# The row of the MLP's inverse roots by two DMA transfers over DRAM, in a hybrid decoder layer on one core

## The chip, the cores and the metric

The kernel runs on one core of a Trainium2 chip. The metric is the device time of one execution in microseconds (us), lower is better.

## The reference

One decoder layer on x of 512 tokens by 1024 channels, in float32. The mixer (block-sparse attention and a gated delta rule side by side) is untouched here. What matters is the second half:

```python
x = x + rms_norm(y, post_norm_mix[l])          # y is the mixer's output
h = rms_norm(x, pre_norm_mlp[l])               # x * rsqrt(mean(x*x) + eps) * gain
y = jnp.square(jax.nn.relu(h @ w_mlp_in[l])) @ w_mlp_out[l]
x = x + rms_norm(y, post_norm_mlp[l])
```

with w_mlp_in 1024 x 4096 and w_mlp_out 4096 x 1024.

## The kernel before, in words

All engines have a program written out by hand, tied together by semaphores. The weights come in units of 128 x 512 elements (256 KB each). SP loads a unit into one of four slots of `raw` (L442), ACT copies it rounded into `w_hi` (`split`, through the helper `copy` on L906), POOL subtracts to get the rest `w_lo` (L1550), and PE multiplies each unit in three passes (hi by hi, hi by lo, lo by hi: L494 to L496 in `three`). The slots are reused with u % 4: ACT's split of unit u waits until PE is done with unit u-4, and runs three units ahead of PE (LEAD = 3).

In the MLP the hidden layer is computed transposed: channels of the hidden layer on the partitions, the 512 tokens along the row. The norm's inverse root is one number for each token, so it isn't applied to h. It is applied after the product, in `relu` on DVE (L1209 by the helper `stt`): `relu_sb = max(bank, 0) * rs_row`. For this `rs_row` must hold the 512 roots as one row of 2 KB, the same on each of the 128 partitions. POOL computes the roots the other way round: `rs2`, 128 partitions by 4, where token t*128+p sits on partition p in column t (`root_x2`: L1543, L1544, then the semaphore `rs2_ready`).

The kernel before turns one into the other in three steps. DVE multiplies the 128 x 128 identity by each column of `rs2` to four diagonal blocks `rs_diag` (L1488, semaphore `diag_ready`). PE multiplies a matrix of ones with `rs_diag` into bank 7 (L847, semaphore `row_full`); the profile shows it as two matmuls. ACT copies bank 7 to `rs_row` (L906, semaphore `row_ready`), and DVE's first relu waits for that.

I number the units of w_mlp_in here as m0, m1, ... (m0 is U_OUT of the code). m0 to m3 are the first block of 256 hidden channels, computed in two halves of the tokens into banks 4 and 5. m4 to m7 are the second block, into banks 2 and 3; each such unit is 12 matmuls of 512 columns. The product with ones stands in PE's program after m6 (`first and j == 2` in `mlp_in`). m8 opens the third block, in banks 0 and 1, and before it PE waits for `relu_done` >= 2, that is for DVE's first two relu instructions, which need `rs_row`.

ACT's program around it (`mlp_in(0, True)`, by its j): splits of m4 and m5 between the squares of x; then j=3 splits m6, j=4 splits m7, j=5 splits m8 (it waits for PE to end m4), j=6 splits m9 (waits for m5), j=7 waits for the product with ones, copies `rs_row`, squares the first two relu results (L1145), then splits m10. On POOL the order is: lo of m4 and m5, the root `root_x2`, lo of m6, and so on. DVE has nothing else to do between the last h_lo and the first relu but the four diagonals. SP's queue carries only the loads of the units there.

Of the kernel before, what the change touches and what calls it, by code (L numbers as in the profile page):

```python
# [16 lines left out]
F32 = mybir.dt.float32  # L17
F32R = mybir.dt.float32r
ALU = mybir.AluOpType
# [3 lines left out]
P = 128  # L23
D = 1024
S = 512
NT = S // P
# [141 lines left out]
def program(nc, x, pre_norm_mix, w_in, conv_w, a_log, dt_bias, dn_norm, w_branch_att, w_branch_dn, w_out,  # L168
# [5 lines left out]
    def at(name, kb, shape, dt=F32):  # L174
        return nc.alloc_sbuf_tensor_at(name, shape, dt, offset=base + int(kb * KB))
# [53 lines left out]
    a_hi = at("a_hi", 176, [P, 4, S], F32R)  # L229
    a_lo = at("a_lo", 184, [P, 4, S], F32R)  # L230
    relu_sb = at("relu_sb", 56, [P, 4, S])
    rs_diag = at("rs_diag", 64, [P, NT, P])
    rs_row = at("rs_row", 66, [P, S])
    y_out = at("y_out", 56, [P, NT, D])

# [2 lines left out]
    def small(name, shape, dt=F32):  # L238
        n = 4
        for d in shape[1:]:  # L240
            n *= d
        t = nc.alloc_sbuf_tensor_at(name, shape, dt, offset=base + off[0])
        off[0] += (n + 31) // 32 * 32
        return t

    ident = small("ident", [P, P])
    neg = small("neg", [P, P])
    ones = small("ones", [P, P])
# [40 lines left out]
    rs2 = small("rs2", [P, NT])  # L289
# [3 lines left out]
    bank = [ctx.enter_context(nc.psum_tensor(f"bank{i}", [P, 512], F32)) for i in range(8)]  # L293
    side = bank[4:]

    def sem(name):
        return ctx.enter_context(nc.semaphore(name))
# [73 lines left out]
    y_scaled = sem("y_scaled")  # L371
    ss2_ready = sem("ss2_ready")
    rs2_ready = sem("rs2_ready")
    diag_ready = sem("diag_ready")
    row_full = sem("row_full")
    row_ready = sem("row_ready")
    t2_full = sem("t2_full")
    t2_hi = sem("t2_hi")
    t2_lo = sem("t2_lo")
# [9 lines left out]
    pool_chain = sem("pool_chain")  # L389

    row_copy = nc.dram_tensor("row_copy", (32, P), F32).ap()
    w1 = w_in[0]
    xt = x[0].rearrange("(t p) d -> t p d", p=P)
    ot = out[0].rearrange("(t p) d -> t p d", p=P)
# [96 lines left out]
    def _(pe):  # L491
# [23 lines left out]
        def unit(u, toks=slice(0, S), done=True, own=None):  # L515
# [3 lines left out]
            if u < U_IN:  # L519
                g = UNIT_GROUP[u]  # L520
                first, banks, _, need = TABLE[g]
                j = u - first
                if GROUPS[g][1] == "f":
# [293 lines left out]
        def mlp_in_unit(s, b, toks):  # L817
            for kk in range(2):
                for m in range(2):
                    c = slice(kk * 256 + m * P, kk * 256 + m * P + P)  # L820
                    k = 2 * s + kk
                    x_ = three(bank[b + m][:, toks], w_hi[:, s, c], w_lo[:, s, c], h_hi[:, k, toks], h_lo[:, k, toks],
                               k == 0, k == KD - 1)
            return x_
# [13 lines left out]
        def mlp_in(i, first):  # L838
            for q in range(1 if first else 0, 2):
                if not first:  # L840
                    pe.wait_ge(relu_done, i * 4 + (2 * q - 2))
                for j in range(4):
                    pe.wait_ge(lo_ready, i * 8 + (U_OUT + 4 * q + j + 1))
                    mlp_in_unit(j, 2 * q, slice(0, S)).then_inc(unit_done, 1)
                    if first and j == 2:
                        pe.wait_ge(diag_ready, NT)
                        pe.matmul(bank[7][:], ones[:], rs_diag[:], start=True, stop=True).then_inc(row_full, 1)  # L847

        mlp_in(0, True)
        with pe.Fori(1, 8) as i:  # L850
            mlp_in(i, False)
# [36 lines left out]
    def _(a):  # L888
        n = {}

        def mark(i, s):

            n[s.name] = n.get(s.name, 0) + 1
            i.then_inc(s, 1)
            a.wait_ge(s, n[s.name])
# [9 lines left out]
        def copy(o, i_, scale=1.0):  # L905
            return a.activation(o, i_, ACT.Copy, scale=scale)  # L906
# [19 lines left out]
        def split(u, slot, loaded, used):  # L926

            a.wait_ge(raw_in[slot], loaded)
            if used is not None:
                a.wait_ge(unit_done, used)  # L930
            copy(w_hi[:, slot, :], raw[:, slot, :]).then_inc(hi_ready, 1)
# [24 lines left out]
        def side_step(name, i):  # L956
# [24 lines left out]
            elif name == "sg":  # L981
                a.wait_ge(conv_done, i + 1)
                dst = qk_dn[:, i, :] if i < 8 else v_dn[:, i - 8, :]
                mark(a.activation(dst, dst, ACT.Silu), silu_done if i < 8 else silu_v_done)
            elif name == "ev" and i in (10, 11):
                first, banks, _, _ = TABLE[i]
                for m, b in enumerate(banks):
                    if m < NT - 1:
# [152 lines left out]
        def square_group(i, q):  # L1141

            for m in range(2):
                a.wait_ge(relu_done, i * 4 + (2 * q + m + 1))
                a.activation(act[:, bass.ds(i * 4 + (2 * q + m), 1), :].rearrange("p a s -> p (a s)"), relu_sb[:, 2 * q + m, :],  # L1145
                             ACT.Square).then_inc(act_ready, 1)

        def mlp_in(i, first, last=False):
            for j in range(8):
                u = U_OUT + LEAD + j  # L1150
                if first and j == 7:
                    a.wait_ge(row_full, 1)
                    mark(copy(rs_row[:], bank[7][:]), row_ready)
                    square_group(i, 0)
                if not (first and j < 3):
                    split(None, u % 4, i * 32 + 16 * (u // 4 + 1), i * 8 + (u - 3))
                if last and j == 5:
                    act_hi(0, 0, False)
                    act_hi(0, 1, False)
                if j in (3, 7) and not (first and j == 3):  # L1160
                    square_group(i, j // 4)

        def act_hi(i, kt, used):

            a.wait_ge(act_ready, i * 4 + (kt + 1) if not isinstance(i, int) else 4 * i + kt + 1)
            if used:
                a.wait_ge(unit_done, i * 8 + (U_M1 + 2 * (kt - 4) + 2))
            copy(a_hi[:, kt % 4, :], act[:, bass.ds(i * 4 + kt, 1), :].rearrange("p a s -> p (a s)")).then_inc(ahi_ready, 1)

        mlp_in(0, True)  # L1170
        with a.Fori(1, 7) as i:
            mlp_in(i, False)
        mlp_in(7, False, True)

        def mlp_out(i, first, last):
# [16 lines left out]
    def _(v):  # L1192
        n = {}

        def mark(i, s):
            n[s.name] = n.get(s.name, 0) + 1
            i.then_inc(s, 1)
            v.wait_ge(s, n[s.name])
# [269 lines left out]
        def h2_part(half, ks):  # L1468
            toks = slice(256 * half, 256 * half + 256)
            for k in ks:  # L1470
                v.wait_ge(t2_hi, half * KD + k + 1)
                mark(stt(h_lo[:, k, toks], bank[k % 4][:, k // 4 * 256:k // 4 * 256 + 256], wmlp[:, k:k + 1],
                         h_hi[:, k, toks].bitcast(F32), ALU.mult, ALU.subtract), t2_lo)
# [9 lines left out]
        h2_part(0, range(6, 8))  # L1483
        residual(3)
        h2_part(1, range(8))
        v.wait_ge(rs2_ready, 1)
        for t in range(NT):
            mark(v.tensor_scalar(rs_diag[:, t, :], ident[:], rs2[:, t:t + 1], None, ALU.mult), diag_ready)  # L1488
        v.wait_ge(row_ready, 1)

        def relu(i, first=False, ms=range(4)):

# [209 lines left out]
```

## Time and profile before

| | us |
|---|---|
| three runs | 785.43, 785.59, 1565.65 |
| their median | 785.59 |
| the profiled execution's own time | 785.03 |
| its span | 783.3 |
| PE busy | 772.8 (99% of the span) |
| ACT, POOL, DVE busy | 354.5, 393.7, 330.5 |
| TensorE's granted clock, mean | 0.998 |

The span is what the profiler saw of the engines; the execution's own time is 1.7 us longer. A number such as L906 is a line of the kernel. PE is the matmul engine, PEld its weight loads, DVE VectorE, ACT ScalarE, POOL GpSimd, SP SyncE; a q behind the name is the engine's instruction queue, where DMAs are issued. Matmuls overlap in the record, so the distance between starts is the pace, not the duration.

### The profile page before, as it was taken

The numbers are of one execution on the slowest core, as the hardware profiler recorded it, in microseconds if no ns is written. First come the engines' busy times: TensorE is split into PE (matmuls) and PEld (weight loads), VectorE is DVE, ScalarE is ACT, GpSimd is POOL, SyncE is SP. The second block draws the span as 40 slices with busy tenths as digits, with TensorE's granted clock in tenths as the row PEclk, the third lists the DMA queues.
The fourth block names the chain that finished last, engine by engine and source line by source line (L and its number), as shares of the span: only waits on it lengthen the run. The fifth ranks groups of instructions, "written<-read, shape, count | busy, mean of one in ns | idle before, by whom it ended". The sixth has DMA issues, their size and how long they took to land.

```text
span 783.3 us, 12452 instructions
## 1 busy us (share of the span) xinstructions
PE 772.8 (99%) x4355; PEld 636.5 (81%) x4355; DVE 330.5 (42%) x502; ACT 354.5 (45%) x633; POOL 393.7 (50%) x347
## 2 busy tenths in 40 slices
PE   9999999999999999999999999999999999999996
PEld 8688788888887878888888888888888888888885
DVE  3596979881463545454507411110113222122225
ACT  6646861268555446445326633333334333333333
POOL 4446994434356343574446454445444544444444
PEclk9999999999999999999999999999999999999999
DMA  6236233323212121223732233333332322332222
GB/s 222 68 94 203 56 82 93 95 81 82 69 41 71 53 69 46 91 77 99 257 97 77 81 95 93 94 107 94 94 93 94 108 95 94 100 100 95 94 80 108
DMA packets 60026, 75.18 MB, mean 96 GB/s; under 512 B 6056, under 2 KB 45008, under 8 KB 59984
## 3 DMA queue, kind: packets, MB, share of 16 engines
q1 hardware_dynamic: 59776, 74.34, 31.5%
q8 instruction: 26, 0.43, 0.2%
q10 hardware_dynamic: 208, 0.28, 0.1%
q14 instruction: 16, 0.13, 0.1%
HBM read 72.49 MB, written 2.11 MB: 95 GB/s over the span
## 4 chain that ended last, share of the span: by engine, by line
PE 95%; DVE 2%; ACT 1%; issue 1%; POOL 1%; DMA 1%; ACTq 0%; DVEq 0%; POOLq 0%
PE bank L494 29%; PE bank L496 28%; PE bank L495 28%; PE bank L706 1%; PE bank L729 1%; PE bank L716 1%; PE bank L619 1%; DVE tmp L1459 1%; DVE y_out L1209 1%; PE bank L670 1%; PE bank L610 1%; PE bank L634 1%; DMA x_sb<-in_x 1%; ACT h_hi L906 1%; PE bank L681 1%
## 5 line engine op out<-in xcount | busy, mean ns | idle before, releaser
L1550 POOL TENSOR_TENSOR w_lo<-raw,w_hi 128x512 fp32r<-128x512 f32 x247 | 320.1, 1302 | 363.2 <-ACT w_hi L906 361.6
L906 ACT ACTIVATE w_hi<-raw 128x512 fp32r<-128x512 f32 (+1 forms) x248 | 155.0, 630 | 260.8 <-PE bank L496 255.2
L494 PE MATMUL bank<-h_hi,w_hi 128*128 128x512 f32 (+1 forms) x576 | 223.2, 387 | 1.5 <-DVE h_lo L1209 1.5
L495 PE MATMUL bank<-h_lo,w_hi 128*128 128x512 f32 (+1 forms) x576 | 217.9, 378 | 0.0
L496 PE MATMUL bank<-h_hi,w_lo 128*128 128x512 f32 (+1 forms) x576 | 217.8, 378 | 0.0
L494 PEld LDWEIGHTS bank<-h_hi,w_hi 128*128 128x128 f32 x576 | 108.6, 188 | 26.3 <-issue 4.6
L496 PEld LDWEIGHTS bank<-h_hi,w_lo 128*128 128x128 f32 x576 | 108.5, 188 | 20.6
L495 PEld LDWEIGHTS bank<-h_lo,w_hi 128*128 128x128 f32 x576 | 108.6, 189 | 18.9 <-issue 0.2
L494 PE MATMUL bank<-w_hi,a_hi 128*128 128x512 f32 x256 | 99.7, 389 | 0.1
L496 PE MATMUL bank<-w_hi,a_lo 128*128 128x512 f32 x256 | 99.6, 389 | 0.0
L495 PE MATMUL bank<-w_lo,a_hi 128*128 128x512 f32 x256 | 99.6, 389 | 0.0
L1502 DVE TENSOR_TENSOR a_lo<-act,a_hi 128x512 fp32r<-128x512 f32 x32 | 40.1, 1255 | 124.0 <-ACT a_hi L906 124.0
L1209 DVE SCALAR_TENSOR_TENSOR relu_sb<-bank,rs_row 128x512 f32<-128x512 f32 x32 | 20.6, 686 | 133.1 <-PE bank L496 130.1
L494 PEld LDWEIGHTS bank<-w_hi,a_hi 128*128 128x128 f32 x256 | 48.1, 188 | 10.4 <-POOL w_lo L1550 0.5
L495 PEld LDWEIGHTS bank<-w_lo,a_hi 128*128 128x128 f32 x256 | 48.1, 188 | 10.0
L496 PEld LDWEIGHTS bank<-w_hi,a_lo 128*128 128x128 f32 x256 | 48.1, 188 | 10.0
L494 PE MATMUL bank<-w_hi,h_hi 128*128 128x512 f32 x128 | 50.3, 393 | 0.1
L495 PE MATMUL bank<-w_lo,h_hi 128*128 128x512 f32 x128 | 49.8, 389 | 0.0
L496 PE MATMUL bank<-w_hi,h_lo 128*128 128x512 f32 x128 | 49.8, 389 | 0.0
L1145 ACT ACTIVATE act<-relu_sb 128x512 f32 (+1 forms) x32 | 19.8, 633 | 43.2 <-DVE relu_sb L1209 42.7
L1050 ACT ACTIVATE probs<-bank,nmax 128x128 f32<-128x128 f32 (+3 forms) x32 | 16.9, 528 | 39.2 <-DVE nmax L1402 38.7
L494 PEld LDWEIGHTS bank<-w_hi,h_hi 128*128 128x128 f32 x128 | 24.0, 188 | 5.6 <-POOL w_lo L1550 0.5
(246 smaller groups left out, 859.5 us busy)
## 6 DMA issues: line engine op xcount, KB each, us to landing
raw<-in_w_in SPq DMA_DIRECT2D x87, 256.0 KB, 2.8
raw<-in_w_mlp_in SPq DMA_DIRECT2D x64, 256.0 KB, 2.7
raw<-in_w_mlp_out SPq DMA_DIRECT2D x64, 256.0 KB, 2.6
raw<-in_w_out SPq DMA_DIRECT2D x16, 256.0 KB, 2.7
decay<-row_copy SPq DMA_DIRECT2D x4, 512.0 KB, 4.2
raw<-in_w_branch_att SPq DMA_DIRECT2D x8, 256.0 KB, 2.8
raw<-in_w_branch_dn SPq DMA_DIRECT2D x8, 256.0 KB, 2.8
x_res<-in_x SPq DMA_DIRECT2D x1, 2048.0 KB, 8.8
```

Of the source, the lines that this page charges most:

```text
L494: pe.matmul(o, s_hi, m_hi, start=start, stop=False, skip_group_check=True)
L495: pe.matmul(o, s_hi, m_lo, start=False, stop=False, skip_group_check=True)
L496: return pe.matmul(o, s_lo, m_hi, start=False, stop=stop, skip_group_check=True)
L610: x_ = pe.transpose(b[:, m * P:(m + 1) * P], src[:, m0 + m, tok], ident[:])
L619: x_ = pe.matmul(two[hh][:, j * 256:j * 256 + 256], qk_dn[r, 4 + q + j, tok], qk_dn[r, q + j::4, tok], start=True, stop=True)
L634: x_ = pe.matmul(b[to, u % 16 * B32:u % 16 * B32 + B32], lhs, rhs, start=True, stop=True)
L906: return a.activation(o, i_, ACT.Copy, scale=scale)
L1050: x_ = a.activation(probs[:, hh, c], side[(f + hh) % 4][:, c], ACT.Exp, bias=nmax[:, hh, j:j + 1], accum_out=psumr[:, hh, j:j + 1])
L1145: a.activation(act[:, bass.ds(i * 4 + (2 * q + m), 1), :].rearrange("p a s -> p (a s)"), relu_sb[:, 2 * q + m, :], ACT.Square).then_inc(ac ...
L1209: return v.scalar_tensor_tensor(out=o, in0=i0, scalar=s, in1=i1, op0=op0, op1=op1)
L1502: v.tensor_tensor(a_lo[:, kt, :], act[:, bass.ds(i * 4 + kt, 1), :].rearrange("p a s -> p (a s)"), a_hi[:, kt, :].bitcast(F32), ALU.subtra ...
L1550: g.tensor_tensor(w_lo[:, slot, :], raw[:, slot, :], w_hi[:, slot, :].bitcast(F32), ALU.subtract).then_inc(lo_ready, 1)
```

## The change

The diagonals, the product with ones and the copy are gone, with `rs_diag` and their three semaphores. Instead ACT, after its split of m6, waits for `rs2_ready` and issues four DMAs. Each stores one column of `rs2` (128 partitions, 4 bytes each) into 512 consecutive bytes of a new scratch row `row2_copy` in DRAM. After its split of m8, ACT waits until all four have landed, and issues one DMA that reads the scratch row of 2 KB into `rs_row` on all 128 partitions (256 KB written). DVE's first relu waits for that one's landing.

```diff
-    rs_diag = at("rs_diag", 64, [P, NT, P])
...
-    diag_ready = sem("diag_ready")
-    row_full = sem("row_full")
-    row_ready = sem("row_ready")
+    row2_out = sem("row2_out")
+    row2_in = sem("row2_in")
...
+    row2_copy = nc.dram_tensor("row2_copy", (1, S), F32).ap()
...
                     mlp_in_unit(j, 2 * q, slice(0, S)).then_inc(unit_done, 1)
-                    if first and j == 2:
-                        pe.wait_ge(diag_ready, NT)
-                        pe.matmul(bank[7][:], ones[:], rs_diag[:], start=True, stop=True).then_inc(row_full, 1)
...
                 if first and j == 7:
-                    a.wait_ge(row_full, 1)
-                    mark(copy(rs_row[:], bank[7][:]), row_ready)
                     square_group(i, 0)
                 if not (first and j < 3):
                     split(None, u % 4, i * 32 + 16 * (u // 4 + 1), i * 8 + (u - 3))
+                if first and j == 3:
+                    a.wait_ge(rs2_ready, 1)
+                    for t in range(NT):
+                        a.dma_start(row2_copy[:, t * P:(t + 1) * P].rearrange("o p -> p o"), rs2[:, t:t + 1]).then_inc(row2_out, 16)
+                if first and j == 5:
+                    a.wait_ge(row2_out, 16 * NT)
+                    a.dma_start(rs_row[:], row2_copy[0].partition_broadcast(P)).then_inc(row2_in, 16)
...
         h2_part(1, range(8))
-        v.wait_ge(rs2_ready, 1)
-        for t in range(NT):
-            mark(v.tensor_scalar(rs_diag[:, t, :], ident[:], rs2[:, t:t + 1], None, ALU.mult), diag_ready)
-        v.wait_ge(row_ready, 1)
+        v.wait_ge(row2_in, 16)
```

## Rows read from the trace of the kernel before

**Rows 1.** The page: shares by engine of the chain that ended last.
```profile
PE 95%; DVE 2%; ACT 1%; issue 1%; POOL 1%; DMA 1%; ACTq 0%; DVEq 0%; POOLq 0%
```

**Rows 2.** Timeline of PE around the product: start us, us, engine, line, op, tiles, count.
```profile
446.49 0.39 PE L496 MATMUL bank<-h_hi,w_lo 128*128 128x512 f32 x1
446.72 1.02 PE L847 MATMUL bank<-rs_diag,ones 128*128 128x512 f32 x2
447.17 0.80 PE L494 MATMUL bank<-h_hi,w_hi 128*128 128x512 f32 x1
447.81 0.40 PE L495 MATMUL bank<-h_lo,w_hi 128*128 128x512 f32 x1
```

**Rows 3.** The chain that ended last, same place: start us, us, what.
```profile
446.88 0.86 PE bank L847 x2
```

**Rows 4.** Waits from 436 to 460 us: us in total, times, longest.
```profile
DVE relu_sb L1209 <- ACT rs_row L906: 3.0, 1, 3.0
ACT rs_row L906 <- PE bank L847: 2.9, 1, 2.9
```

**Rows 5.** Timelines of POOL (first two rows) and DVE, 440 to 452 us.
```profile
440.35 1.01 POOL L1544 TENSOR_TENSOR rs<-ss,nhalf 128x4 f32<-128x4 f32 x1
441.61 5.04 POOL L1550 TENSOR_TENSOR w_lo<-raw,w_hi 128x512 fp32r<-128x512 f32 x4 [0.25 <-POOL rs L1544]
...
441.47 4.02 DVE L1488 TENSOR_SCALAR rs_diag<-ident,rs 128x128 f32<-128x128 f32 x4 [5.73 <-POOL rs L1544]
448.47 1.29 DVE L1209 SCALAR_TENSOR_TENSOR relu_sb<-bank,rs_row 128x512 f32<-128x512 f32 x2 [2.98 <-ACT rs_row L906]
450.54 1.29 DVE L1209 SCALAR_TENSOR_TENSOR relu_sb<-bank,rs_row 128x512 f32<-128x512 f32 x2 [0.79 <-PE bank L496]
```

**Rows 6.** Timeline of PEld: the first weight load of m8.
```profile
450.12 0.19 PEld L494 LDWEIGHTS bank<-h_hi,w_hi 128*128 128x128 f32 x1
```

**Rows 7.** Timeline of ACT: splits m6 and m7, m8, m9, and the copy.
```profile
439.68 1.15 ACT L906 ACTIVATE w_hi<-raw 128x512 fp32r<-128x512 f32 x2
441.54 0.63 ACT L906 ACTIVATE w_hi<-raw 128x512 fp32r<-128x512 f32 x1 [0.70 <-PE bank L496]
444.26 0.63 ACT L906 ACTIVATE w_hi<-raw 128x512 fp32r<-128x512 f32 x1 [2.09 <-PE bank L496]
447.77 0.60 ACT L906 ACTIVATE rs_row<-bank 128x512 f32<-128x512 f32 x1 [2.89 <-PE bank L847]
```

**Rows 8.** Timelines: the DMA issues on ACT's queue, and one on SP's.
```profile
0.80 0.42 ACTq L909 DMA_DIRECT2D x_sb<-in_x  x1
1.25 0.59 ACTq L910 DMA_DIRECT2D wpre_rows<-in_pre_norm_mix  x1
...
60.35 0.32 ACTq L978 DMA_DIRECT2D row_copy<-c_rows  x1
...
10.22 0.44 SPq L459 DMA_DIRECT2D alog<-in_a_log  x1
```

**Rows 9.** DMA issues: tiles, queue, count, KB each, median us from issue to landing.
```profile
raw<-in_w_mlp_in SPq DMA_DIRECT2D x64, 256.0 KB, 2.7
decay<-row_copy SPq DMA_DIRECT2D x4, 512.0 KB, 4.2
...
out<-y_out SPq DMA_DIRECT2D x2, 256.0 KB, 2.0
...
wmlp<-in_pre_norm_mlp SPq DMA_DIRECT2D x1, 4.0 KB, 4.3
...
row_copy<-c_rows ACTq DMA_DIRECT2D x1, 16.0 KB, 1.4
```

**Rows 10.** Busy time by stretch; the last three numbers are clock, DMA share, GB/s.
```profile
438.00:444.00 6.00, 6.00 (x31) 5.04 (x30) 2.46 (x3) 3.43 (x6) 5.25 (x6) 1.00 0.31 87
444.00:449.00 5.00, 5.00 (x22) 3.78 (x21) 1.99 (x3) 1.23 (x2) 2.65 (x3) 1.00 0.71 207
```

**Rows 11.** DMA queues from 59 to 62 us: packets, MB, share of 16 engines.
```profile
q10 hardware_dynamic: 48, 0.02, 2.8%
```

## The prediction

> **What bounds the kernel now.** I read the page first. The chain that ended last is 95% PE [rows 1], at the granted clock 1.00, so only what makes PE work less or wait less can shorten the kernel. Then the timelines of the engines around 447 us, where the changed lines stand, and the table of waits there. It has two entries of the old route, DVE for the copy 3.0 us and ACT for the product 2.9 us [rows 4]. Neither is a wait of PE, so neither is on the chain. What is on it is the product itself: the chain gives L847 0.86 us for its two matmuls [rows 3]. The timeline agrees. The last matmul of m6 starts at 446.49 and at a pace of 0.23 us the next would start at 446.72. With the product in between, the first matmul of m7 begins late and slowly (0.80 us long), and its second one starts at 447.81 [rows 2]. 447.81 less one pace is 447.58, against 446.72: again 0.86 us.
>
> **The parts, one by one.**
>
> *Taken from PE: two matmuls, -0.86 us.* This is the only removed work on the chain. From 450 us on PE is paced by its own matmuls and the others follow it, so a gain here moves everything behind it forward, if the wait below stays hidden.
>
> *Taken from DVE: four diagonals, 4.02 us from 441.47 [rows 5]. Taken from ACT: the copy of 0.60 us at 447.77 [rows 7].* Both are off the chain. They matter only as the old route: roots ready at 441.36 (440.35 + 1.01), relu at 448.47 [rows 5], which is 7.1 us. The old route is paced by PE's program order (the product stands behind m6), not by its own 5.5 us of work.
>
> *Added: the new route.* It has a deadline. PE needs the first two relus before it loads the first weights of m8. Before, that was 450.12 [rows 6] and the relus were done at 448.47 + 1.29 = 449.76: 0.36 us to spare. Without the product PE is there at 450.12 - 0.86 = 449.26. So the relus must start by 449.26 - 1.29 = 447.97, some 0.5 us earlier than in the kernel before. The gain takes its own cover away: with the relus starting at 448.47 as before, 0.50 of the 0.86 would be lost again. Every microsecond after 447.97 is a microsecond of PE.
>
> Now the route, from 441.36.
> 1. ACT is free (its splits of m6 and m7 end at 440.83, m6's alone about 440.3 [rows 7]) and waits. The first store is issued at about 441.45, as the diagonals started at 441.47.
> 2. Four issues. On ACT's queue one took 0.42 us with 0.45 to the next, others 0.59 and 0.32; on SP one with 128 tiny rows took 0.44 [rows 8]. I take 0.48 from one to the next, by the row nearest in shape. The fourth is issued at 442.9 and ACT is free at 443.35. Bounds: 0.32 to 0.63 each, so the fourth between 442.4 and 443.35.
> 3. The landing of the fourth store. No row shows stores of 4 bytes. The nearest is the other scratch store, 16 KB in rows of 512 bytes from the same queue: 1.4 us; a 256 KB store took 2.0, and the slowest tiny transfer, behind others at the start of the kernel, 4.3 [rows 9]. Each DMA engine gets 8 elements of each store and a semaphore write, 36 packets in all. The other store's 48 packets took 2.8% of 16 engines over 3 us, 28 ns each [rows 11], so 36 are 1.0 us spread over the 1.5 us of the issues: no queue builds up at that price. Below 1.4 us is not excluded, but gives nothing, since ACT is then still busy (step 4). I take 2.0 us, between the scratch store and the doubt about the small elements: landed at 444.9. Bounds 1.4 to 4.3: 444.3 to 447.2.
> 4. Meanwhile ACT splits m7 (443.4 to 443.95) and m8 (to 444.5; PE is done with m4 long before). The wait for the stores is thus 0.4 us long in my case.
> 5. The broadcast is issued at 444.95. The nearest row is a load of a unit, also 256 KB: 2.7 us; the read of the other scratch row, twice as large, took 4.2 [rows 9]. The DMA engines are 71% busy from 444 to 449 [rows 10], by four unit loads. Two of these will come later than now, since POOL's lo of m7 comes later (below). I take 2.8 us: landed at 447.75. Bounds 2.0 (no row of a load is shorter than that store) to 4.2.
> 6. The relus start at 447.75 + 0.1 = 447.85, against the deadline of 447.97: hidden, by only 0.1 us.
>
> *Moved: ACT's splits.* m7 ends at 443.95 in place of 440.83, m8 at 444.5 in place of 442.17, m9 at 446.0 in place of 444.89. Behind them POOL: its four lo parts ran from 441.61 to 446.65 [rows 5], 1.26 each. Now m6 to 442.87, m7 from 444.05 to 445.3, m8 to 446.6, m9 to 447.9. PE loads weights for m7 at 446.5, for m8 at 449.3, for m9 at 452: spare 1.2, 2.7 and 4. With the slowest issues (0.63 each) m7's lo ends at 445.9, still in time. SP's loads for the slots of m7 and m8 (units m11, m12) go out about 1.2 us later and are needed by ACT only at 452 and later. So the moves cost nothing; if that cover were gone, m7's lateness would be a stall of its own length.
>
> The sum on the profiled execution: 785.03 - 0.86 = 784.17. The median of the runs is 0.56 above it, so 784.73. As the margin is 0.1 us with errors of several tenths in each of two landings, I add a little and forecast **784.8**.
>
> **A page of the Trainium skill, weighed.** The trace has the scratch store at 1.4 us from issue to landing [rows 9]. The Trainium skill, "DMA: Bandwidth & Descriptors", section "Anatomy of one DMA", puts a fixed cost of about 2.0 us on any DMA, most of it the confirmation of the write, and warns of a long delay where the target is HBM. It is given for the GpSimd path, and the row is below it. By it, as an estimate, the store lands at 444.9 and the broadcast (2.0 + 0.6 for 256 KB) 2.6 us after its issue, so that the relus would start at 447.65 and nothing changes in the sum. The same page, section "Specifications", says that transfers under 512 bytes are done as read-modify-write. That speaks against this change, and it is the page's side of the rivals B and C below; no row shows such a write to DRAM, and how much one costs can't be had from the page.
>
> **The rivals.**
>
> *B. Hidden in part.* The relus start between 447.97 and 448.83. Say the stores land after 2.6 us (445.5) and the broadcast takes 2.9: relus at 448.5, stall 0.5, net -0.3, about 785.2. For it: the engines at 71% [rows 10], and the decay reads' 4.2. Against: the loads of that same stage keep their 2.7.
>
> *C. The wait takes over: slower.* PE stands before m8 for longer than 0.86 us. It decides at relus from 448.83 on, that is a route from 441.36 longer than 7.5 us. With the stores at 3.0 us (445.9), the broadcast at 4.2 (445.9 + 4.2 = 450.1): relus at 450.2, stall 2.2, net +1.4, about 787.0. With both at the upper bounds: 447.2 + 4.2 + 0.1 = 451.5, stall 3.5, net +2.7, 788.3. For it: 128 elements of 4 bytes written into the same 512 bytes by 16 engines, which no row shows, and contention with the unit loads. Against: 28 ns a packet and 1.4 us for the only scratch store.
>
> *D. The small stores run one after another.* If each packet began only when the one before had landed (1.4 less the issue of 0.3 is 1.1 us), 36 of them are 40 us: relus near 485, time near 821, slower by 4.5%. Against: 32 rows landed in 1.4 us in the row of the trace, so two on an engine can't have cost 1.1 each.
>
> *E. It gains nothing, as PE's slot isn't given back.* Where PE waits for something else right behind the product, for instance m7's lo part (spare 1.2 by my count): 785.6. Against: the pace of m7 and m8 in the trace is unbroken.
>
> **How the numbers follow.** A 0.50 (784.2 to 784.9, own range with the spread of the runs 783.9 to 785.0), B 0.22, C 0.22, D 0.02, E 0.04. The range goes from 783.9 to 787.5: below it hardly anything, above it D and the upper third of C. A measurement of this kernel tells 2% (15.7 us) from no change, and nothing in A, B, C or E comes near: faster by over 2% 0.01, within 2% 0.96, slower by over 2% 0.03.
>
> **What would show it.** In the changed profile: no L847, PE's pace of 0.23 us unbroken from m6 to m7; ACT's queue with four issues about 0.48 apart from 441.45; splits of m7 and m8 ending near 444.0 and 444.5; the broadcast's issue near 444.95 and the first relu near 447.85; no idle time of PE before m8. If the relu starts later than 447.97, PE shows idle time before m8 "waiting for DVE relu_sb" of just that length; a landing of the stores over 3 us, or of the broadcast over 4, makes the forecast wrong. If the relus wait for something other than the broadcast, the reasoning about the route is wrong.

## The result, and the profile after

The changed kernel takes 794.84 us (median of four runs, 794.23 to 795.66), against 785.51 for the kernel before: ratio 1.0124, 95% interval 1.0111 to 1.0136. That is 9.3 us slower, where 0.8 us less was forecast; the time lies above the range. (Of the four runs of the kernel before one took 1565.65 us; it is in this median, 785.43 without it, and not in the ratio.) The profiled execution took 795.66 us with a span of 794.0, so the spans differ by 10.7 us.

The product is gone from PE, as told. What took its place stands in the chain of the changed kernel (start us, us, what):

```profile
443.18 7.88 DMA row_copy<-rs
...
451.08 5.50 DMA rs_row<-row_copy
...
456.67 0.17 DVE relu_sb L1210
...
457.28 0.69 DVE relu_sb L1210
...
458.10 0.79 PE bank L493
```

Before, the chain ran through PE alone here [rows 3]. Now it runs from POOL's roots through both transfers and DVE's relus. The fourth store landed 7.88 us after its issue, the broadcast 5.50 us after its own, and the relus started at 456.67 in place of 448.47 [rows 5]. The waits of the stage (436 to 475 us) say who stood for it (us in total, times, longest):

```profile
DVE relu_sb L1210 <- DMA rs_row<-row_copy: 20.5, 1, 20.5
...
PE bank L493 <- DVE relu_sb L1210: 8.1, 1, 8.1
...
ACT w_hi L902 <- DMA row_copy<-rs: 6.6, 1, 6.6
```

DVE's 20.5 us cost nothing in themselves, since it has no other work. PE's 8.1 us are the price. ACT's queue went as forecast up to the wait for the stores (the issues 0.45 us apart, m7 and m8 split at once behind them):

```profile
441.83 1.80 ACTq L1154 DMA_DIRECT2D row_copy<-rs  x4
443.74 1.15 ACT L902 ACTIVATE w_hi<-raw 128x512 fp32r<-128x512 f32 x2 [2.98 <-issue]
451.08 0.33 ACTq L1157 DMA_DIRECT2D rs_row<-row_copy  x1
451.51 0.63 ACT L902 ACTIVATE w_hi<-raw 128x512 fp32r<-128x512 f32 x1 [6.62 <-DMA row_copy<-rs]
```

And the busy time by stretch (the columns as in [rows 10]; the third number from the end is the granted clock) shows a second loss:

```profile
450.00:452.00 2.00, 0.04 (x1) 0.00 (x0) 0.00 (x0) 0.49 (x1) 0.00 (x0) 1.00 0.38 68
452.00:454.00 2.00, 0.00 (x0) 0.00 (x0) 0.00 (x0) 0.14 (x1) 1.26 (x1) 0.93 0.87 115
454.00:456.00 2.00, 0.00 (x0) 0.00 (x0) 0.00 (x0) 0.00 (x0) 0.00 (x0) 0.50 0.97 265
...
458.00:460.00 2.00, 1.90 (x5) 1.52 (x6) 1.16 (x2) 2.00 (x5) 0.78 (x1) 0.50 0.00 0
460.00:465.00 5.00, 5.00 (x15) 3.93 (x14) 0.00 (x0) 1.34 (x3) 2.44 (x3) 0.61 0.36 106
465.00:475.00 10.00, 10.00 (x45) 8.26 (x45) 1.29 (x2) 2.99 (x6) 3.20 (x3) 1.00 0.27 81
```

PE stood from 450, the granted clock fell to 0.50 (1.2 GHz, where 1.00 is 2.4 GHz) while it stood, and it was at 1.00 again only some 6 us after PE had restarted. Three rows of PE's timeline fix the size:

```profile
449.66 0.39 PE L495 MATMUL bank<-h_hi,w_lo 128*128 128x512 f32 x1
458.10 0.79 PE L493 MATMUL bank<-h_hi,w_hi 128*128 128x512 f32 x1 [8.05 <-DVE relu_sb L1210]
...
464.35 0.40 PE L493 MATMUL bank<-h_hi,w_hi 128*128 128x512 f32 x1
```

The next matmul was due at 449.66 + 0.23 = 449.88 and came at 458.10: 8.22 us. From there to 464.35 are 15 matmuls; they took 6.25 us and would have taken 15 x 0.227 = 3.40 at the higher clock: 2.85 us more. (This is the slowest of the four runs.) The roots were ready at 441.80 and not at 441.36, 0.44 us later for reasons ahead of the change. So 0.44 + 8.22 + 2.85 - 0.86 = 10.65, of the 10.7 by which the spans differ.

### The profile page after: what moved, and what is told of

Same layout as the page of the kernel before. It is cut to its first block, busy times and chain, and to the rows that moved or that the text cites. A ratio compares the mean times of both kernels' runs of the same rounds, so it can differ in the third digit from the quotient of the medians.

```text
span 794.0 us, 12446 instructions
## 1 busy us (share of the span) xinstructions
PE 775.4 (98%) x4353; PEld 638.5 (80%) x4353; DVE 326.5 (41%) x498; ACT 353.3 (44%) x632; POOL 393.8 (50%) x347
## 4 chain that ended last, share of the span: by engine, by line
PE 92%; DMA 2%; DVE 2%; ACT 2%; issue 1%; POOL 1%; ACTq 0%; DVEq 0%; POOLq 0%
PE bank L493 28%; PE bank L494 27%; PE bank L495 27%; PE bank L705 1%; PE bank L728 1%; PE bank L715 1%; DMA row_copy<-rs 1%; PE bank L618 1%; ACT h_hi L902 1%; DVE tmp L1460 1%; DMA rs_row<-row_copy 1%; DVE y_out L1210 1%; PE bank L669 1%; PE bank L609 1%; PE bank L633 1%
## 5 line engine op out<-in xcount | busy, mean ns | idle before, releaser
L1210 DVE SCALAR_TENSOR_TENSOR relu_sb<-bank,rs_row 128x512 f32<-128x512 f32 x32 | 20.5, 686 | 153.1 <-PE bank L495 132.6
```

The lines of the kernel that those rows point to most:

```text
L1210: return v.scalar_tensor_tensor(out=o, in0=i0, scalar=s, in1=i1, op0=op0, op1=op1)
```

## The experiments

All are variants of the changed kernel unless said otherwise. Where the broadcast reads x in place of the scratch row, or stores are left out or moved, the row of roots holds other numbers, and nothing else differs. "Before" is the time of the kernel before on the same chip. All but E11, E13 and E14 are single runs, and so are their kernels before except for E9, E10 and E12. The same kernel before ran from 783.82 to 785.72 us in 21 runs, so a difference of under 1 us between single runs says nothing; the landings in the traces carry these experiments.

**E1, another row is read.**

```diff
-                    a.dma_start(rs_row[:], row2_copy[0].partition_broadcast(P)).then_inc(row2_in, 16)
+                    a.dma_start(rs_row[:], x[0][0, 0:S].partition_broadcast(P)).then_inc(row2_in, 16)
```

> As the changed kernel, but the broadcast reads the first 2 KB of x and not the scratch row (so the row of roots holds other numbers, the work is the same). In the changed kernel the broadcast took 5.5 us from issue to landing, where the unit loads of the kernel before took 2.7. If reading lines that were just written is what is slow, the broadcast lands here after 2.7 to 3.5 us and the time is 2 to 3 us shorter (about 792). If 128 reads of one row are slow in themselves, or the engines are held up by something else, it stays at 5 to 6 us and the time at 794 to 795.7.

Measured 794.82 us (before 784.95). The chain:

```profile
441.87 8.60 DMA row_copy<-rs
...
450.49 5.98 DMA rs_row<-in_x
```

Reading lines just written isn't what makes the broadcast slow. E2 to E7, E9, E10 and E12 keep this edit. The stores were the same as in the changed kernel, and the fourth landed after 8.60 us and not 7.88 (in E11 after 8.61): so far apart do landings of the same stores lie.

**E2, one store of four.**

```diff
-                    for t in range(NT):
+                    for t in range(1):
...
-                    a.wait_ge(row2_out, 16 * NT)
+                    a.wait_ge(row2_out, 16)
```

> As E1, but only the first of the four stores is made (128 elements of 4 bytes and not 512) and waited for; the other three columns are left out. Theory M: the elements are written one after another at one place, about 16 ns each (8.4 us from the first packet to the landing over 512 elements), so 128 take about 2.1 us plus some 1.4 for issue and start: landing 3 to 4 us after its issue. Rival F: a fixed delay of a small store to DRAM, about 7 us, whatever the number: landing again after 7. Time by M about 786 to 788, by F about 792 to 794.

Measured 792.57 us (before 784.95). The one store took about as long as the last of four:

```profile
441.28 8.14 DMA row_copy<-rs
```

So M, 16 ns for each of 512, is wrong in that form. F stands so far.

**E3, the elements 512 bytes apart.**

```diff
-    row2_copy = nc.dram_tensor("row2_copy", (1, S), F32).ap()
+    row2_copy = nc.dram_tensor("row2_copy", (S, 128), F32).ap()
...
-                        a.dma_start(row2_copy[:, t * P:(t + 1) * P].rearrange("o p -> p o"), rs2[:, t:t + 1]).then_inc(row2_out, 16)
+                        a.dma_start(row2_copy[t * P:(t + 1) * P, 0:1], rs2[:, t:t + 1], allow_slow_non_contiguous=True).then_inc(row2_out, 16)
```

> As E1, with all four stores, but each element of 4 bytes goes to an address 512 bytes from the last (a scratch of 256 KB and not 2 KB). Theory M says the 512 elements of the changed kernel are slow because they meet in the same lines of DRAM: spread out they land in 2 to 3 us, the stall before m8 falls to 0 to 3 us and the clock stays at 1.00. Rival N: every 4-byte store to DRAM costs this, wherever it goes, by its number alone: the landing stays near 7.9 us after the fourth issue.

Measured 784.42 us (before 784.95), with the same number of packets of 4 bytes into DRAM. Chain and landings:

```profile
442.65 1.81 DMA row_copy<-rs
444.48 3.60 DMA rs_row<-in_x
448.17 1.30 DVE relu_sb L1210 x2
```

The same 512 small writes land in 1.81 us in place of 7.88 when they don't stand side by side. Neither their number nor their size is the cause alone, nor DRAM as the target: it is their addresses. Up to the landing this kernel is the forecast come true, with the fourth store at 442.65 and its landing at 444.46 (forecast 442.9 and 444.9). The broadcast then took 3.60 us and not 2.8, the relus started at 448.17 (forecast 447.85), and PE lost a little, which no table of waits shows but its timeline does:

```profile
449.08 0.39 PE L495 MATMUL bank<-h_hi,w_lo 128*128 128x512 f32 x1
449.60 0.49 PE L493 MATMUL bank<-h_hi,w_hi 128*128 128x512 f32 x1
```

The first matmul of m8 came 0.52 us behind the last of m7 and not 0.23. It is no usable kernel, since a row so spread out can't be read back as one row.

**E4, the elements into SBUF.** The stores go to a second tile of 128 x 4 there.

```diff
-    row2_copy = nc.dram_tensor("row2_copy", (1, S), F32).ap()
+    row2_copy = at("row2_sb", 64, [P, NT])
```

> As E1, but the four stores of 128 elements of 4 bytes go to a second tile in SBUF (same partitions) and not to DRAM. If DRAM as the target is the cause (M or N), they land within 2 us and the loads of m9 to m12 keep their 2.7 us. If many tiny packets are the cause, with any target, they land after 7 us again.

Measured 785.92 us (before 784.95). The issues were slower (0.62 us apart), the fourth landed 2.65 us after its issue, a little over what was expected, and the relus started at 449.70:

```profile
443.09 2.65 DMA row_sb<-rs
445.76 3.85 DMA rs_row<-in_x
```

PE waited 1.7 us before m8, and the loads of the stage (440 to 460 us) landed after 3.2 us. Tiny packets by themselves aren't slow as in the changed kernel. (Here too no two elements stand side by side, so E4 alone doesn't tell the target from the addresses; E3 does.)

**E5, E9 and E10, the elements 64, 16 and 8 bytes apart.** The edit is E3's, with `(S, 16)`, `(S, 4)` and `(S, 2)`.

> As E3, but the elements of 4 bytes go 64 bytes apart (a scratch of 32 KB, each column's 128 elements in 8 KB). E2 showed that 128 adjacent elements alone need 8.1 us, so the cost isn't shared over all 512. Theory M2: elements that meet in one small stretch of DRAM are written one after another, about 55 ns each, and different stretches side by side. If the stretch is 64 bytes or smaller, these land like E3's (1.8 us) and the time is about 784.5. If the stretch is 512 bytes (8 elements meet now, not 128), the landing is 0.4 us later than E3's. If it is larger still (several KB), the landing is again near 8 us and the time near 794.

> As E5, with the elements of 4 bytes 16 bytes apart (a scratch of 8 KB): 4 of them meet in each 64 bytes and 32 in each 512. So far, from the first issue to the last landing: 9.2 us for 512 adjacent elements, 8.1 for 128, 6.0 for 32 (two stretches of 64 bytes), against 3.2 at 512 bytes apart and 3.8 at 64. Theory L: writes that meet in one stretch of 64 bytes go one after another at some 0.3 us each, stretches side by side; 16 meeting cost 4.6 to 6. Then 4 meeting cost 1.2 to 1.6: the last landing is at 4.2 to 5.0 us from the first issue, the time 785.5 to 787. Rival: what counts is 512 bytes or the number in all; then 32 or 512 meeting give 6 to 9 us again, 789 to 794.

> As E9, 8 bytes apart: 8 elements meet in each 64 bytes. Theory L: 2.4 to 3.2 us on top of some 3.2, so the last landing 5.5 to 6.5 us from the first issue, about halfway between E9 and the changed kernel. Rival: as with adjacent elements, 9 us.

Measured 785.27 us (before 785.3), 789.38 and 789.82 (before 784.23, the median of seven). From the chains of the three, the landing of the fourth store:

```profile
442.82 2.47 DMA row_copy<-rs
```
```profile
443.15 4.27 DMA row_copy<-rs
```
```profile
443.32 3.96 DMA row_copy<-rs
```

E5 landed 0.66 us later than E3, where 0 or 0.4 was expected. E9 and E10 took 5.6 and 5.3 us from the first issue to the last landing.

**E6 and E12, 32 and 31 adjacent elements in one store.**

```diff
-                    for t in range(NT):
-                        a.dma_start(row2_copy[:, t * P:(t + 1) * P].rearrange("o p -> p o"), rs2[:, t:t + 1]).then_inc(row2_out, 16)
+                    a.dma_start(row2_copy[:, 0:32].rearrange("o p -> p o"), rs2[0:32, 0:1]).then_inc(row2_out, 16)
```

(E12 has 31 in both places; in both kernels ACT waits for 16.)

> As E2, but the one store has 32 elements in 128 adjacent bytes (32 partitions, the other 96 left out). M2, one after another at 55 ns: about 1.8 us for the elements and 1.4 for the rest, landing at 3 to 3.5 us. Rival F, a fixed penalty of adjacent small stores whatever their number: landing at about 8 us again, as with 128 and with 512 elements.

> As E6, but 31 adjacent elements of 4 bytes and not 32 (partitions 0 to 30). The Trainium skill, DMA: Bandwidth & Descriptors, section on why a DMA increments its semaphore by 16, says that a DMA is split over as many engines, up to 16, as divide the count of its rows; 31 is prime, so one engine writes all 31, where E6's 32 were written by 16 engines, two each. The packets in the trace show it (31 and one semaphore write, against 32 and 16). Theory X: writes of different engines into the same stretch are what is slow; then these land within 1.5 to 2.5 us of the issue. Rival Y: each small write into a stretch waits for the one before, whoever writes it; then 5 to 7 us as in E6.

Measured 789.65 us (before 785.3) and 789.15 (before 784.88). Landings, E6 and then E12:

```profile
441.77 5.98 DMA row_copy<-rs
```
```profile
441.46 5.91 DMA row_copy<-rs
```

and ACT's DMA queue from 442 to 444 us (packets, MB, share), E6 and then E12:

```profile
q10 hardware_dynamic: 48, 0.00, 1.2%
```
```profile
q10 hardware_dynamic: 32, 0.00, 0.9%
```

48 are 32 and 16 semaphore writes, 32 are 31 and one: a single engine wrote E12's, and it made no difference. These counts are as the Trainium skill has the split over the engines in "DMA: Bandwidth & Descriptors", in its section on why a DMA increments its semaphore by 16. Theory X, engines that get in each other's way, falls. Neither of E6's two theories gave its 6 us (3 to 3.5, or 8). In all, from the first issue to the last landing:

| kernel | elements | bytes apart | in each 64 bytes | us |
|---|---|---|---|---|
| E3 | 512 | 512 | 1 | 3.2 |
| E5 | 512 | 64 | 1 | 3.8 |
| E9 | 512 | 16 | 4 | 5.6 |
| E10 | 512 | 8 | 8 | 5.3 |
| E6, E12 | 32, 31 | 4 | 16 | 6.0, 5.9 |
| E2 | 128 | 4 | 16 | 8.1 |
| changed kernel, E1, E11 | 512 | 4 | 16 | 9.2, 10.0, 10.0 |

Two things are shown. Elements of 4 bytes 64 bytes apart or more land fast (3.2 and 3.8 us), those 16 bytes apart or less slowly (5.3 us and more), and 31 of them by one engine suffice; where between 16 and 64 bytes the line lies, no run shows. Beyond that the cost doesn't follow a simple count: 16 times as many elements (512 against 32) cost 1.6 times as much, and that 8 meeting cost no more than 4 is within the 0.8 us by which the same stores differ (9.2 and 10.0). Theory L missed both of its ranges: E9 by 0.6 us above, E10 by 0.2 below. How the memory handles such writes stays open.

**E7, no stores.** The four stores and ACT's wait for them are left out.

> As E1 with the four stores and the wait for them left out: after the roots are ready and m7 and m8 are split, ACT issues the broadcast at once (of the first row of x). It lands after 2.7 to 3.6 us if the 5.5 to 6.0 us of the changed kernel and of E1 are after-effects of the stores; after 5 to 6 us if 128 reads of one 2 KB row are slow in themselves. In the first case the row is there before PE's deadline and the time is 0.5 to 0.9 us under the kernel before: 784.1 to 784.5.

Measured 784.21 us (before 785.3). The landings of the stage (KB each, median us):

```profile
raw<-in_w_mlp_in SPq DMA_DIRECT2D x9, 256.0 KB, 2.7
rs_row<-in_x ACTq DMA_DIRECT2D x1, 256.0 KB, 3.0
```

The broadcast of a row to 128 partitions takes 3.0 us, near the 2.8 of the forecast. Its 5.5 to 6.0 us in the changed kernel and in E1 are after-effects of the stores, and so are the loads' (440.5 to 460 us of the changed kernel):

```profile
raw<-in_w_mlp_in SPq DMA_DIRECT2D x5, 256.0 KB, 8.8
```

E7's broadcast is issued earlier than theirs, at 441.47, but those of E3, E5 and E13, issued from 444.48 to 445.32 behind quick stores, took no more than 3.3 to 3.6 us either. Whether the stores slow the broadcast directly or through the held-up loads that it meets, no run separates.

**E8, the kernel before with the four stores added,** after ACT's split of m6 as in the changed kernel; the wait for them stands at ACT's end.

> The kernel before (diagonals, product and copy stay, the output is the reference's), with the four stores of 128 adjacent 4-byte elements added at the same place of ACT's program; nobody waits for them before the end. It shows what they do to the others. If they only take their own time, the loads of m9 to m12 keep 2.7 us and the time stays at 785.0 to 785.6 (ACT's splits come 2 us later, which is covered). If they hold up the DMA engines for all (the loads took 8 to 10 us in the changed kernel), these loads land late, ACT's splits of m10 to m12 wait for them, and PE may stall by 0 to 4 us: 785 to 789.

Measured 784.74 us (before 785.3). The landings, and the waits:

```profile
raw<-in_w_mlp_in SPq DMA_DIRECT2D x8, 256.0 KB, 5.9
...
row_copy<-rs ACTq DMA_DIRECT2D x4, 0.5 KB, 7.3
```
```profile
ACT w_hi L908 <- DMA raw<-in_w_mlp_in: 6.5, 2, 4.1
```

They hold up the unit loads, and ACT waited 6.5 us for units. PE waited 0.6 us for POOL's lo of one. The rest was covered by the three units of lead. So the damage to the neighbours is real and cost too little here for a single run to show; the wait for the row is what costs.

**E11, PE kept busy while it waits.**

```diff
         mlp_in(0, True)
+        for _ in range(34):
+            pe.matmul(bank[7][:], h_hi[:, 0, 0:P], h_hi[:, 0, :], start=True, stop=True)
         with pe.Fori(1, 8) as i:
```

> The changed kernel with 34 more matmuls (128x128 by 128x512, h_hi by h_hi into bank 7, used by nobody) in PE's program between m7 and its wait before m8. At 0.227 us each they fill 7.7 of the 8.05 us in which PE stood. They add no waiting of their own as long as they end before the relus. In the changed kernel the granted clock fell to 0.50 during the stall and came back only 6 us after PE's restart; 13 matmuls ran at 0.43 us a piece. If the stall brought the lower clock, it stays at 1.00 here and 13 x 0.20 = 2.6 us are won: 792.0 to 792.6. If the clock falls for another reason (the transfers, the time of the stage), it stays at 794.3 to 795.5.

Measured 792.56 us, ratio to before 1.0101 (1.0084 to 1.0118); the changed kernel's is 1.0124. The stage:

```profile
449.28 7.87 PE L847 MATMUL bank<-h_hi 128*128 128x512 f32 x34
458.23 0.49 PE L493 MATMUL bank<-h_hi,w_hi 128*128 128x512 f32 x1 [1.09 <-DVE relu_sb L1212]
458.56 0.40 PE L494 MATMUL bank<-h_lo,w_hi 128*128 128x512 f32 x1
```

The stores and the broadcast are as slow as ever, the relus start at 456.81, m8 at 458.23, but its matmuls run at 0.23 us from the second on. The span is 791.3 against 794.0, 2.7 us less; the medians differ by 2.3. The lower clock came with PE's standing, not with the transfers.

**E13, rows of 128 bytes.** DVE turns the roots round before the stores. It computes what the reference does.

```diff
...
+        link(v.memset(rs2_w[:], 0.0))
+        v.wait_ge(rs2_ready, 1)
+        link(v.tensor_copy(rs2_w[:, 0:NT], rs2[:]))
+        mark(v.transpose(rs2_t[:], rs2_w[:]), rs2_turned)
...
-                    a.wait_ge(rs2_ready, 1)
+                    a.wait_ge(rs2_turned, 1)
...
-                        a.dma_start(row2_copy[:, t * P:(t + 1) * P].rearrange("o p -> p o"), rs2[:, t:t + 1]).then_inc(row2_out, 16)
+                        a.dma_start(row2_copy[0].rearrange("(j q) -> j q", q=P)[:, t * B32:(t + 1) * B32], rs2_t[B32 * t:B32 * t + NT, :]).then_inc(row2_out, 16)
```

> The changed kernel with the roots turned round on DVE first (a copy to a 32-wide tile and a transpose in blocks of 32 x 32), so that the four stores write 4 rows of 128 bytes each, 16 rows in all, in place of 512 elements of 4 bytes. The output is the reference's. If stores below the size of a stretch are the cause, these land within 2 us of the last issue; with 0.5 us for DVE, 1.8 for the issues and 3 to 3.6 for the broadcast, the relus start at 448.2 to 449, 0.2 to 1.0 us after PE's deadline of 447.97, and the time is that of the kernel before, within -0.7 and +0.2 us. If adjacency alone does it, whatever the row's length, they land after 5 to 8 us and the time is 789 to 794.

Measured 784.60 us (before 784.88), ratio to before 0.9997 (0.9988 to 1.0007). ACT's queue, and DVE's relus:

```profile
442.57 1.29 ACTq L1157 DMA_DIRECT2D row_copy<-rs_t  x4
443.97 1.15 ACT L905 ACTIVATE w_hi<-raw 128x512 fp32r<-128x512 f32 x2 [3.00 <-issue]
444.75 0.35 ACTq L1160 DMA_DIRECT2D rs_row<-row_copy  x1
...
448.14 1.29 DVE L1213 SCALAR_TENSOR_TENSOR relu_sb<-bank,rs_row 128x512 f32<-128x512 f32 x2 [5.60 <-DMA rs_row<-row_copy]
```

The stores had landed by 444.75, at most 2.2 us after the first issue, and ACT never waited for them. The broadcast took 3.3 us, the relus started at 448.14, and PE's matmuls follow each other without a gap from m6 to m8. So the same 2 KB filled in 16 rows of 128 bytes do no harm. The four rows of one store lie 512 bytes apart, and a row's neighbours come with the next stores, some 0.3 us apart; rows between 4 and 128 bytes long, or neighbours within one store, no run shows. The same two transfers are some 10 us better this way. By the trace the 0.86 us of the product are gained; the runs don't resolve it (0.3 in the medians, the interval has both no gain and 0.9), so the kernel is no better than the one before within what was measured.

**E14, no row at all.** It computes what the reference does.

```diff
-                stt(relu_sb[:, m, :], bank[4 + m if first and m < 2 else m][:], 0.0, rs_row[:], ALU.max, ALU.mult).then_inc(relu_done, 1)
+                v.tensor_scalar(relu_sb[:, m, :], bank[4 + m if first and m < 2 else m][:], 0.0, None, ALU.max).then_inc(relu_done, 1)
...
+            link(g.tensor_scalar(ss2[:], ss2[:], 1.0 / D, EPS, ALU.mult, ALU.add))
+            link(g.tensor_tensor(eps2[:], ss2[:], ss2[:], ALU.mult))
+            link(g.tensor_scalar(eps2[:], eps2[:], EPS, None, ALU.mult))
...
-            link(g.tensor_scalar(ssh[:, t:t + 1], ssy[:, 2 * t:2 * t + 1], EPS, None, ALU.add))
+                link(g.tensor_tensor(ssh[:, t:t + 1], ssy[:, 2 * t:2 * t + 1], eps2[:, t:t + 1], ALU.add))
```

(The last line is for the MLP's norm only. The diagonals, the product and the copy go as in the change, and no transfer takes their place.)

> The kernel before without the row: the root is the same factor r for all channels of a token, it comes out of the relu and of the square as r squared, and the last norm divides by the root of the mean square; so r cancels but for eps, which becomes eps / r^4 = eps * (mean(x*x) + eps)^2 for each token. POOL computes that in place of the root (three tiny operations), and adds it in place of eps. The diagonals, the product, the copy and the relu's factor are gone; no transfer is added. On PE's chain the 0.86 us of the product go and no wait comes, since the relu waits for PE alone. Expected: 0.86 us less than the kernel before, ratio 0.9989, the relus of m0 to m3 at once after these units and not at 448.47. Rival: PE's slot isn't given back, 0 us.

Measured 784.04 us against 784.88, ratio 0.9988 (0.9979 to 0.9997): 0.8 us less, where 0.86 was worked out. It is the only kernel here whose gain stands clear of its interval, and by little.

## Why the prediction was wrong

**Right:** the product's 0.86 us. E14, which takes it away and adds nothing, gives 0.84 less in the medians, and E7 1.1 in one run. Right too were the place where the wait would bite (PE before m8), the issues (0.45 for 0.48), the splits of m7 and m8, and that their moving costs nothing. The deadline was right as well, better than the waits in the tables show. In the kernel before, the weights of m8 are loaded as the last matmul of m7 starts (450.12 both), so each kernel has its own deadline: that start less 1.29 us for two relus.

| kernel | deadline | relus | late | lost | lost less 0.86 | measured |
|---|---|---|---|---|---|---|
| E3 | 447.79 | 448.17 | 0.38 | 0.39 | -0.5 | -0.5 |
| E5 | 447.98 | 449.02 | 1.04 | 1.05 | +0.2 | 0.0 |
| E4 | 447.77 | 449.70 | 1.93 | 1.94 | +1.1 | +1.0 |
| E13 | 448.56 | 448.14 | no | 0 | -0.9 | -0.3 |

"Lost" is how much later the first two matmuls of m8 start than at 0.227 us apart, "measured" the time against the kernel before. E3 to E5 are single runs, so that the last two columns agree this closely is in part luck.

**Wrong, step 3: the landing of the fourth store.** Taken at 2.0 us with 4.3 as the upper end, it took 7.88. The error has a form worth seeing. I priced the stores by what the DMA engines spend on a packet, 28 ns, and concluded that no queue builds up. That much came true, at even less a packet. ACT's DMA queue from 442 to 445 us of the changed kernel:

```profile
q10 hardware_dynamic: 576, 0.00, 10.2%
```

All 576 packets (512 and 64 semaphore writes) are in these 3 us, at 8.5 ns each by their share (10.2% of 16 engines over 3 us), and the stores landed 6 us after that. The time lies behind the last packet of the queue, and no duration of a store's packet shows it. The nearest row, 32 rows of 512 bytes in 1.4 us, was near in its target and in its queue but not in what mattered, the length of a row: each of its rows fills 512 bytes of its own. Rival C named the right circumstance (many 4-byte elements into the same bytes), but its upper bound, 4.3 us from the rows at hand, was too low by nearly half; rival D's chain of single landings at 1.1 us each was far too high.

**Wrong, step 5: the broadcast.** Taken at 2.8 us, at most 4.2, it took 5.50. E7 shows 3.0 without the stores. The step took the transfers as independent but for bandwidth. Even behind stores that landed in time it was a little short: 3.6 in E3 and E5, 3.3 in E13. With a margin of only 0.1 us in step 6, that alone put E3's relus past the deadline; so the forecast of no wait at all would have missed by some 0.4 us of wait even if step 3 had held. From 445 to 451 us ACT's queue has no packets, and SP's queue moved, in the changed kernel and then in the kernel before:

```profile
q1 hardware_dynamic: 332, 0.32, 53.5%
```
```profile
q1 hardware_dynamic: 860, 0.82, 46.3%
```

A higher busy share for under half of the bytes: by their share the packets took 155 ns each (332 of them) against 52 (860).

**Missing: the clock.** "Every microsecond after 447.97 is a microsecond of PE" held for E3, E4 and E5 (1.7 us of wait), whose granted clock stayed at 1.00 in every stretch. After waits of 3.0 us and more it didn't. This is E6, first a stretch, then PE's timeline:

```profile
451.00:456.00 5.00, 2.77 (x7) 2.21 (x8) 2.48 (x4) 3.31 (x6) 1.37 (x2) 0.75 0.19 60
```
```profile
449.58 0.39 PE L495 MATMUL bank<-h_hi,w_lo 128*128 128x512 f32 x1
453.23 0.60 PE L493 MATMUL bank<-h_hi,w_hi 128*128 128x512 f32 x1 [3.27 <-DVE relu_sb L1209]
...
456.98 0.39 PE L493 MATMUL bank<-h_hi,w_hi 128*128 128x512 f32 x1
```

The first matmul of m8 came 3.42 us late. From it to 456.98 are 9 matmuls in 3.75 us, where 9 x 0.227 = 2.04 were due: 1.7 us more. With the -0.86 that makes 4.3, and its time is 4.35 us over the kernel before. Counted in the same way the clock cost 1.7 us in E9, E10 and E12 (waits of 3.0 to 3.2 us; their times are 5.2, 5.6 and 4.3 us over), 1.8 in E2 (6.5), 2.1 in E1 (9.3) and 2.85 of the 10.65 in the changed kernel (8.1): the cost didn't grow in step with the wait. The mechanism was rival C: the row comes late and PE stands before m8. C's prices for the stores and the broadcast were both short, and the clock it didn't have.

**The read-modify-write.** The remark of the Trainium skill on transfers below 512 bytes ("DMA: Bandwidth & Descriptors", section "Specifications") pointed the right way, and I gave it no weight in the sum because no row priced it. The Trainium skill gives 512 bytes as the least size for the full rate; for the time to the landing the runs don't draw the line there: rows of 128 bytes (E13) landed within 2.2 us of their first issue. Elements of 4 bytes that stood alone in their 64 bytes landed within 3.2 and 3.8 us of the first of four issues (E3, E5).

## What to carry to other kernels

Before a column is stored to DRAM as a row, turn it round on the chip, so that each write is a row of 128 bytes or more; a copy and a transpose in blocks of 32 x 32 cost 0.4 us on DVE here (E13) and made the landing some 6 us earlier. No length between 4 and 128 bytes was tried. A transfer whose kind no row shows deserves an upper bound by the time to its landing, not by its packets, and where a chain with 0.1 us to spare hangs on it, that bound belongs in the forecast; here even the bound, 4.3 us, was short of 7.88. And ask first whether the value is needed where it is applied: the factor that three engines laid out as a row cancels in the next norm but for eps.

## What the runs showed of the hardware that was not expected

- One store of 31 elements of 4 bytes to adjacent addresses in DRAM, by one DMA engine, lands after 5.9 us (E12); 512 elements 512 bytes apart land 1.8 us after the last issue (E3).
- While such writes are under way, loads of other data by another queue land after 8.8 us (changed kernel) or 5.9 (E8), in the median, and not after 2.6 to 2.7.
- In the four kernels in which PE waited 3.0 to 3.3 us (E6, E9, E10, E12) a stretch at half the clock followed that cost 1.7 us more; in E4 (1.7 us) none did. In the changed kernel the clock was back 6 us after the restart.
- Stores of single elements from SBUF to SBUF were issued 0.62 us apart (E4), those to DRAM 0.45 (the changed kernel).
